# A two-block transformer kernel: the value product of the cross-attention moved behind the query product with the softmax inside it, and a one-block product that keeps its own bank parity

## What is computed

```python
def memory_cross_attention(hn, mem_n, w_q, w_kv, w_o):
    q = (hn @ w_q).reshape(B, S, CROSS_HEADS, CROSS_HEAD)
    k, v = split_cols_2(mem_n @ w_kv, (CROSS_HEADS * CROSS_HEAD, CROSS_HEADS * CROSS_HEAD))
    ...
    s = jnp.einsum('bshd,bmhd->bhsm', q, k).astype(jnp.float32) * (CROSS_HEAD ** -0.5)
    prob = jax.nn.softmax(s, axis=-1).astype(v.dtype)
    o = jnp.einsum('bhsm,bmhd->bshd', prob, v).reshape(B, S, CROSS_HEADS * CROSS_HEAD)
    return o @ w_o
```

## Time and profile before

| | |
|---|---|
| median of 3 runs | 2597.48 us (2597.47 to 2599.82) |
| the profiled execution | 2600.32 us, of which its span in the trace is 2598.5 us |
| PE busy | 2432.8 us, 94% of the span |
| DVE, ACT busy | 1391.4 us (54%), 1097.9 us (42%) |
| mean granted clock of PE | 0.964 of full speed |
| memory traffic | 492.46 MB read, 191 GB/s over the span |

### The profile page before, as it was taken

How to read it: one execution, slowest core, us unless ns; L and a number is a source line. 1 busy time by engine, 2 the same in 40 slices (tenths; PEclk the granted TensorE clock), 3 DMA queues, 4 the chain that set the end, 5 groups by cost and what they waited for, 6 DMA issues and landing times.

```text
span 2598.5 us, 29841 instructions
## 1 busy us (share of the span) xinstructions
PE 2432.8 (94%) x12196; PEld 1935.8 (74%) x12196; DVE 1391.4 (54%) x1302; ACT 1097.9 (42%) x1106; POOL 45.0 (2%) x74
## 2 busy tenths in 40 slices
PE   5799999999989899999999887999899999999996
PEld 0486778887568788877877666787788888888885
DVE  0245345456936787566456765654545545445443
ACT  1355535343334444545344623345534434434332
POOL 0000000001000000000000000000000000000000
PEclk7799999999989999999999988999999999999998
DMA  9945445557956596654555001554455555555552
GB/s 390 369 145 191 149 134 164 176 189 293 420 216 228 202 381 214 209 178 155 175 178 162 27 17 30 212 183 156 130 188 185 184 194 189 189 193 185 193 194 98
DMA packets 231536, 498.00 MB, mean 192 GB/s; under 512 B 29240, under 2 KB 31304, under 8 KB 222064
## 3 DMA queue, kind: packets, MB, share of 16 engines
q1 hardware_dynamic: 224976, 459.44, 52.0%
q0 software_dynamic: 6432, 36.72, 3.8%
HBM read 492.46 MB, written 3.67 MB: 191 GB/s over the span
## 4 chain that ended last, share of the span: by engine, by line
PE 63%; DVE 5%; ACT 2%; DMA 2%; issue 1%; DVEq 0%; POOL 0%; ACTq 0%
PE banks L2325 55%; PE banks L2395 2%; DMA raw_eight<-in_w_ada 1%; PE banks L2692 1%; ACT weights_hi L718 1%; DVE weights_lo L1378 1%; PE banks L2751 1%; PE banks L2570 1%; PE banks L2533 1%; DVE inverse_products L2109 1%; PE banks L2516 0%; DVE inverse_by_chunk L2110 0%; DVE residual L1731 0%; DVE residual L1736 0%; PE banks L2666 0%
## 5 line engine op out<-in xcount | busy, mean ns | idle before, releaser
L1378 DVE TENSOR_TENSOR weights_lo<-weights_raw,weights_hi 128x2048 fp32r<-128x2048 f32 (+1 forms) x364 | 816.5, 2244 | 899.1 <-ACT weights_hi L718 896.6
L718 ACT ACTIVATE weights_hi<-weights_raw 128x2048 fp32r<-128x2048 f32 (+1 forms) x364 | 683.3, 1878 | 1062.3 <-PE banks L2325 1045.0
L2325 PE MATMUL banks<-weights_hi,acts_hi 128*128 128x512 f32 (+1 forms) x2240 | 887.7, 396 | 31.7 <-ACT gate_rank_T L731 10.1
L2325 PE MATMUL banks<-weights_lo,acts_hi 128*128 128x512 f32 (+1 forms) x2240 | 876.0, 391 | 0.0
L2325 PE MATMUL banks<-weights_hi,acts_lo 128*128 128x512 f32 (+1 forms) x2240 | 875.7, 391 | 0.0
L2325 PEld LDWEIGHTS banks<-weights_hi,acts_hi 128*128 128x128 f32 x2240 | 424.5, 190 | 135.2 <-issue 27.7
L2325 PEld LDWEIGHTS banks<-weights_hi,acts_lo 128*128 128x128 f32 x2240 | 424.3, 189 | 88.3
L2325 PEld LDWEIGHTS banks<-weights_lo,acts_hi 128*128 128x128 f32 x2240 | 425.0, 190 | 85.7 <-issue 1.2
L2325 PE MATMUL banks<-weights_hi,hidden_hi 128*128 128x512 f32 x320 | 124.9, 390 | 0.0
L2325 PE MATMUL banks<-weights_hi,hidden_lo 128*128 128x512 f32 x320 | 124.5, 389 | 0.0
L2325 PE MATMUL banks<-weights_lo,hidden_hi 128*128 128x512 f32 x320 | 124.5, 389 | 0.0
(11 more groups left out here) (503 smaller groups left out, 1947.0 us busy)
## 6 DMA issues: line engine op xcount, KB each, us to landing
weights_raw<-in_w_in_e SPq DMA_DIRECT2D x80, 1024.0 KB, 5.3
raw_eight<-in_w_ada SPq DMA_DIRECT2D x72, 1024.0 KB, 16.0
weights_raw<-in_w_up SPq DMA_DIRECT2D x64, 1024.0 KB, 5.7
weights_raw<-in_w_down SPq DMA_DIRECT2D x64, 1024.0 KB, 5.1
weights_raw<-in_w_in SPq DMA_DIRECT2D x44, 1024.0 KB, 5.1
weights_raw<-in_w_in_o SPq DMA_DIRECT2D x32, 1024.0 KB, 5.7
weights_raw<-in_w_out_e SPq DMA_DIRECT2D x16, 1024.0 KB, 5.4
gate_chunks<-in_w_ada POOLq DMA_DIRECT2D x16, 1024.0 KB, 7.6
```

Source lines behind the costliest of these rows:

```text
L718: eng.activation(WHI[:, c % 2, :, 0:n], RAW[:, sl, :, 0:n], ACT.Copy).then_inc(hi_ready, 1)
L1378: eng.tensor_tensor(WLO[:, c % 2, :, 0:n], RAW[:, c % 4, :, 0:n], WHI[:, c % 2, :, 0:n].bitcast(F32), ALU.subtract).then_inc(lo_ready, 1)
L2325: ins = eng.matmul(BANKS[:, par * 2 + h, 0:s.n], x[:, t, h * P:(h + 1) * P], w[:, c % 2, k, 0:s.n], start=(kc == 0 and k == 0 and m == 0), ...
```

## The change

It is made of two parts.

**Block numbers.** A stage is still rounded up to an even number of blocks where its end would be odd, except `att1`, `cross_k` and `cross_q`. `lora` now is an odd block, in banks 2 and 3, and `rkv` starts with an even one. No instruction moves by this on any engine; only banks and semaphore counts differ.

**Cross-attention.** `cross_kv` is cut into `cross_k` and `cross_v`, and `cross_q` stands between them. The transposes of K stay inside `cross_q`. Those of Q, all four units of scores and the transposes of the first two units of probabilities stand on PE inside `cross_v`, the softmax on ACT and DVE there too. Behind `cross_v` remain two units of transposes, all four products with V, and their split. `cross_probs_T` has a slot for each unit, and the four small buffers stand elsewhere.

```diff
@@ stages
-        Stage("cross_kv", wv(a["w_kv_cross"][0], 0, D, 0, NB), 2, x=(XTH2, XTL2), acts="memT", scale=2, dest=lambda b, h: CKV[:, bass.ds(b, 1), h, :]),
+        Stage("cross_k", wv(a["w_kv_cross"][0], 0, D, 0, NB), 1, loop=False, x=(XTH2, XTL2), acts="memT", scale=2,
+              dest=lambda b, h: CKV[:, 0, h, :]),
         Stage("cross_q", wv(a["w_q_cross"][0], 0, D, 0, NB), 1, loop=False, acts="x3T", scale=4, ahead=2, dest=lambda b, h: CQ[:, 0, h, :]),
+        Stage("cross_v", wv(a["w_kv_cross"][0], 0, D, NB, NB), 1, loop=False, x=(XTH2, XTL2), acts="memT", scale=2, ahead=2,
+              dest=lambda b, h: CKV[:, 1, h, :]),
...
-        b += s.nblk + s.nblk % 2
+        s.pad = 0 if s.name in ("att1", "cross_k", "cross_q") else (b + s.nblk) % 2
+        b += s.nblk + s.pad
...
-                        evac(s, b, b % 2)
+                        evac(s, b, (s.b0 + b) % 2)
@@ ACT
-        stream(st["cross_q"], after={3: lambda: (rms_squares(XN, 4, Y), tiles_out("ckT", CKT))})
-        tiles_out("cqT", CQT)
+        stream(st["cross_q"], after={0: x3_hi(4, 5), 1: x3_hi(6, 7), 3: lambda: (rms_squares(XN, 4, Y), tiles_out("ckT", CKT))},
+               following=st["cross_v"])
...
+        stream(st["cross_v"], after={1: lambda: tiles_out("cqT", CQT), 2: lambda: units(cross_exp, 0, 1),
+                                     3: lambda: (units(cross_exp, 2, 3), units(cross_probs_copy, 0, 1))}, hold=True)
+        values_out = held.pop()
+        hi(st["cross_o"], st["cross_o"].g0, 0, 0)
+        values_out()
+        units(cross_probs_copy, 2, 3)
+        units(cross_hi, 0, 1, 2, 3)
+        stream(st["cross_o"])
@@ DVE
+        stream(st["cross_q"], after={0: x3_lo(4, 5), 1: x3_lo(6, 7), 3: lambda: inverse_rms(4)}, following=st["cross_v"])
+        lo(st["cross_v"], st["cross_v"].g0, 0, 1)
...
+        stream(st["cross_v"], after={2: lambda: (units(cross_max, 0, 1), units(cross_divide, 0, 1)),
+                                     3: lambda: (units(cross_max, 2, 3), units(cross_divide, 2, 3))})
+        lo(st["cross_o"], st["cross_o"].g0, 0, 0)
+        units(cross_lo, 0, 1, 2, 3)
@@ PE
-        stream(st["cross_kv"], after={1: x3_tiles(0, 1, 2, 3), 3: x3_tiles(4, 5), 4: x3_tiles(6, 7)})
+        stream(st["cross_k"], after={1: x3_tiles(0, 1, 2, 3), 2: x3_tiles(4, 5), 3: x3_tiles(6, 7)})
...
+        stream(st["cross_v"], after={0: cross_queries, 1: all_scores, 2: lambda: units(cross_probs, 0, 1)})
+        units(cross_probs, 2, 3)
+        eng.wait_ge(block_out, 4 + 2 * st["cross_o"].b0)
+        units(cross_outputs, 0, 1, 2, 3)
```

More of the change, by code:

```diff
@@ L737, in evac @@
                 eng.activation(s.dest(i, h), src, func, scale=scale)\
-                   .then_inc(block_out, 3 if h == 1 and s.nblk % 2 else 1)
+                   .then_inc(block_out, 3 if h == 1 and s.pad else 1)
         held = []
@@ L1313, in _ @@
                                  10: memory_hi(0, 1), 11: memory_hi(2, 3), 12: memory_hi(4, 5), 13: memory_hi(6, 7)})
[L1314 to L1317 removed]
+        stream(st["cross_k"], after={2: lambda: rms_squares(MEMN, 2, Y), 3: x3_hi(0, 1, 2, 3)}, following=st["cross_q"])
+        stream(st["cross_q"], after={0: x3_hi(4, 5), 1: x3_hi(6, 7), 3: lambda: (rms_squares(XN, 4, Y), tiles_out("ckT", CKT))},
+               following=st["cross_v"])
         def cross_exp(u):
@@ L1332, in cross_probs_copy @@
         def cross_probs_copy(u):
-            if u >= 2:
-                bank_full(eng, J[f"cross_o{u - 2}"])
             jj = J[f"cross_p{u}"]
             bank_full(eng, jj)
-            free(eng.activation(CPT[:, u % 2, :], bank(jj), ACT.Copy), jj)
+            free(eng.activation(CPT[:, u, :], bank(jj), ACT.Copy), jj)
         def cross_tiles(t, u):
@@ L1347, in cross_hi, with units @@
             ch.done("cross_hi")
-        def cross_attention():
-            for step, u in ((cross_exp, 0), (cross_exp, 1), (cross_exp, 2), (cross_probs_copy, 0), (cross_exp, 3),
-                            (cross_probs_copy, 1), (cross_probs_copy, 2), (cross_hi, 0), (cross_probs_copy, 3),
-                            (cross_hi, 1), (cross_hi, 2), (cross_hi, 3)):
-                step(u)
-        stream(st["cross_o"], after={0: cross_attention})
+        def units(step, *us):
+            return [step(u) for u in us]
+        stream(st["cross_v"], after={1: lambda: tiles_out("cqT", CQT), 2: lambda: units(cross_exp, 0, 1),
[6 more added lines that the diff above has]
+        stream(st["cross_o"])
         first_up = st["up0"]
@@ L2241, in _ @@
                       10: memory_lo(0, 1), 11: memory_lo(2, 3), 12: memory_lo(4, 5), 13: memory_lo(6, 7)}, hold=True)
-        second = st["cross_q"]
-        stream(st["cross_kv"], after={2: lambda: inverse_rms(2), 3: x3_lo(0, 1, 2, 3), 5: x3_lo(4, 5), 6: x3_lo(6, 7)},
-               following=second)
-        lo(second, second.g0, 0, 1)
-        stream(st["cross_q"], after={3: lambda: inverse_rms(4)})
+        stream(st["cross_k"], after={2: lambda: inverse_rms(2), 3: x3_lo(0, 1, 2, 3)}, following=st["cross_q"])
+        lo(st["cross_q"], st["cross_q"].g0, 0, 1)
+        stream(st["cross_q"], after={0: x3_lo(4, 5), 1: x3_lo(6, 7), 3: lambda: inverse_rms(4)}, following=st["cross_v"])
+        lo(st["cross_v"], st["cross_v"].g0, 0, 1)
         def cross_max(u):
@@ L2358, in stream @@
                 acts_ready(s, kt)
-                chunk(s, None, b % 2, kc, g, g, kt, s.kc)
+                chunk(s, None, (s.b0 + b) % 2, kc, g, g, kt, s.kc)
                 if c in after:
@@ L3005, in _, with cross_queries @@
         stream(st["cross_q"], after={1: cross_keys})
-        eng.wait_ge(block_out, 4 + 2 * st["cross_o"].b0)
-        transposes("cqT", natural(CQ))
-        jobs_out(eng, "cqT")
+        def cross_queries():
+            eng.wait_ge(block_out, 4 + 2 * st["cross_v"].b0)
+            transposes("cqT", natural(CQ))
         def cross_scores(u):
@@ L3036, in cross_outputs, with units, all_scores @@
                     ins = eng.matmul(bank(jj)[:, e * P:(e + 1) * P], CKV[:, 1, sh, g * P:(g + 1) * P],
-                                     CPT[:, u % 2, (2 * e + sh) * P:(2 * e + sh + 1) * P], start=(sh == 0),
+                                     CPT[:, u, (2 * e + sh) * P:(2 * e + sh + 1) * P], start=(sh == 0),
                                      stop=(sh == 1))
             full(ins, jj)
-        for u in range(4):
-            cross_scores(u)
-        for step, u in ((cross_probs, 0), (cross_probs, 1), (cross_probs, 2), (cross_outputs, 0), (cross_probs, 3),
-                        (cross_outputs, 1), (cross_outputs, 2), (cross_outputs, 3)):
-            step(u)
+        def units(step, *us):
+            return [step(u) for u in us]
+        def all_scores():
+            jobs_out(eng, "cqT")
+            units(cross_scores, 0, 1, 2, 3)
+        stream(st["cross_v"], after={0: cross_queries, 1: all_scores, 2: lambda: units(cross_probs, 0, 1)})
+        units(cross_probs, 2, 3)
+        eng.wait_ge(block_out, 4 + 2 * st["cross_o"].b0)
+        units(cross_outputs, 0, 1, 2, 3)
         stream(st["cross_o"], after={2: x4_tiles(0, 1), 3: x4_tiles(2, 3)})
```

26 lines of the change are left out of this document (10 added, 16 removed).

## The result

The changed kernel takes **2583.79 us** (median of four runs, 2582.68 to 2586.69) against 2597.83 us for the kernel before on the same chip (2597.47 to 2599.82): ratio 0.9946, 95% interval 0.9929 to 0.9963. The gain is 14.0 us where 18.2 were forecast; the range of 2577 to 2585 holds the time. The profiled execution took 2586.69 us with a span of 2584.9 us, against 2598.5 before: 13.6 us.

What follows compares the result with a forecast made beforehand. PE, busy for 94% of the span, was taken as the bound, so only its idle or slow time counts. Gains of 8.45 and 9.7 us sum to 18.2, from 2597.5 to 2579.3 us; range 2577 to 2585.

Steps and rivals of the forecast that it cites:

- The two stops: PE's waits from `att1` to `lora` and `lora` to `rkv`: removing them and the slow matmuls behind gains 8.45 us.
- the sign: Between `lora` and `rkv`: `rkv`'s first matmul starts within 0.8 us of `lora`'s last, at full speed.
- The replaced 22.2 us: PE's stretch from `cross_q` to `cross_o`: 22.2 us give way to 12.5 us, a gain of 9.7 us.
- The wait ahead of `cross_v`: Ahead of `cross_v`'s first chunk PE waits 0.6 us for K's copies and the split.
- Q's transposes: Eight transposes of Q between the chunks of `cross_v` cost PE 0.9 us.
- scores: The 16 records of scores on PE inside `cross_v` cost 3.7 us, as they stand.
- probabilities: Transposes of two units of probabilities on PE cost 0.9 us.
- the end: Behind `cross_v`: V's copy with eight transposes, 32 records of products with V and the last split cost 6.4 us.
- The softmax not hidden: Exponentials hold up a split in `cross_v` and PE waits: 2582.5 to 2584.5 us, both failures 2586; chance 0.07.
- one part brings nothing: Either part fails: 2587.8 us without the first, 2589.0 without the second; chance 0.05.
- The clock falling inside `cross_v`: Short transposes and scores between `cross_v`'s chunks let the clock fall: 28 us more, 2607 us; chance 0.04.
- the gain is given back: At a later wait that doesn't move with PE, the gain is lost: 2597.5 us; chance 0.03.

Runs made afterwards that it cites:

- the block numbers' kernel: Kernel before with the change's block numbers alone, cross-attention as before: 2592.75 us, ratio 0.9979; run once more, 2592.83 us, ratio 0.9967.
- the single filler: Changed kernel plus one fp32 128x512 matmul on constants behind the second half of the corner products, ahead of the solve: 2578.5 us, ratio 0.9913.
- the changed kernel's second run: The changed kernel once more, nothing altered, in a later group: 2585.34 us, ratio 0.9936 to the kernel before.
- 5.4 with three: Changed kernel plus three fp32 128x512 matmuls on constants, one and two behind the halves of the corner products: 2580.51 us, ratio 0.9927.
- 9.1 with three in the kernel before: Kernel before plus three filler matmuls, one behind the first and two behind the second half of the corner products: 2597.51 us, ratio 0.9988.

## Why the prediction was right, and where it was off

**The two stops: right.** Forecast 8.45 us, measured 8.41 less the 0.29 that lay ahead, 8.1. The first stop went whole (0.23 us from start to start), at the second 0.49 us of idle time stayed for `weights_lo` where 0.56 was forecast, and that split was indeed what is late next. `rkv` starts 0.81 us behind `lora`'s last matmul, at the edge of the 0.8 that the sign allowed.

**The replaced 22.2 us: right, and by its terms.** The wait ahead of `cross_v` 0.6 (1786.36 less 1785.54 and 0.23; forecast 0.6), Q's transposes 0.87 (0.9), scores 3.45 (3.7), probabilities 0.87 (0.9), the end 6.54 (6.4: V's copy 1.52, products 3.84, last split 1.18). Sum 12.3 where 12.5 stood; the lead grew by 10.1 us where 9.7 stood. The softmax hid with 1.3 us of room at V's fourth chunk where 1.6 was forecast.

**The rivals.** The softmax not hidden did not come; the experiment with the softmax behind V shows what the cover is worth, 6.6 us. That one part brings nothing is excluded by the two kernels with one part each (6.4 and 11.2 us). The clock falling inside `cross_v` did not come: 1.00 from 1786 to 1820 us. For that rival the Trainium skill ("TensorE: Matmul & The Clock Gate", "A second HAM failure mode: psum-queue depth-cycling") was weighed; by that rule the stretch would have run partly low. It didn't; but the rows above show no idle moment between its groups, so the rule's condition was not met, and this run says nothing against it.

**What was off: the sum.** It added the two local gains and took all that lies behind as unchanged: "the gain is given back" had a chance of 0.03, because I looked for "no long stop of PE behind either place". The loss is no stop. It is a stretch of PE work that runs at the lower clock level for longer, 4.8 us from R0 to the first `a_rb_T` product (leads 8.26 and 3.47), some 300 us behind the first place. The other terms, 8.1 and 10.1 us, give with the 0.3 us that lay ahead of the change 18.5; less 4.8 this is 13.7, and 13.6 were measured in the spans. The forecast's time was therefore 4.5 us low, and its bounds of 2577.8 to 2583.4, made of the bounds of the local terms alone, missed the 2583.79; the range held it by luck, because it reached out for another rival.

Could it have been seen in the trace of before? The prediction says of the clock: "I see it fall only behind stops near 3 us". That reading was wrong. The windows behind the first place are:

```profile
1440.00:1500.00 60.00, 50.30 (x233) 35.44 (x231) 45.88 (x84) 35.39 (x68) 1.07 (x2) 0.88 0.04 12
1500.00:1560.00 60.00, 52.56 (x376) 40.39 (x376) 35.71 (x65) 19.62 (x43) 5.25 (x2) 0.84 0.08 18
1560.00:1620.00 60.00, 46.65 (x700) 38.00 (x701) 35.42 (x74) 23.98 (x63) 1.89 (x2) 0.89 0.14 33
```

Ahead of the solve it fell at 1604.5 us, in an idle time of 1.52 us, with none above 0.70 us in the 20 us before; from 1659 to 1663 us it is at 0.57 with PE recorded busy for all 4.00 us. The rows also have the place: the clock at 0.56 and 0.58 from 1604 to 1612 us, and then the 96 records of small matmuls of the solve. They don't say that the low stretch would last 20 us if it began 10 us earlier. But a cost for "the low stretch there gets longer" could have been bounded: with every small matmul at half the clock, by this estimate at most their 5.9 us once more. That bound was missing.

**What stays open.** Why the low stretch lasts some 20 us where R0 starts 4.88 to 5.16 us behind the fall, and 7 or 10 us where it starts earlier or later, the runs do not tell; only that PE was recorded busy for all of 1604 to 1612 us in both executions of the block numbers' kernel. The Trainium skill ("TensorE: Matmul & The Clock Gate", "What's actually happening") says that the monitor behind the clock runs free and doesn't start anew with a kernel, so that the place of a change of level differs between executions. The two executions of one program agree with that: R0 starts 5.38 us behind the fall in one and 4.88 in the other. Nor is it settled how much of the 6.8 us in the medians is the single filler's. Its trace, set against that of the changed kernel's second run, gains 5.6 us up to the first `a_rb_T` product, loses 1.5 again ahead of the memory's transposes, and gains 1.6 between 1870 and 1901 us. The last is the clock again, far from the filler; these are the windows of the changed kernel's second run and of the one with a filler:

```profile
1870.00:1874.00 4.00, 4.00 (x13) 3.12 (x12) 0.74 (x1) 0.00 (x0) 0.00 (x0) 0.60 0.97 334
1870.00:1874.00 4.00, 4.00 (x19) 3.34 (x18) 2.05 (x1) 1.92 (x1) 0.00 (x0) 1.00 0.38 146
```

Both traces of the block numbers' kernel are without that loss too, and no run tells whether the filler had a part in it.

## What to carry to other kernels

Sum the local gains of a change, and then look at each later stretch in which PE runs small matmuls around a fall of the granted clock: where such a stretch lies against the clock's steps can cost or return several microseconds, here 3.3 between two executions of one program and 4.8 of some 18 that the edit brought. If a program's times fall into two groups, compare a trace of each before explaining the median. A full-width matmul on constants put into an existing wait of PE (here 1.69 us, ahead of the solve) cost 0.2 us of lead, took the stretch from R0 to the state product from 13.27 to 8.48 us, and came with a median 6.8 us lower, half of what the whole change brought. It is worth a try beside such a stretch. That it makes times steadier is not shown: they spread over 2.4 us with one filler, 5.4 with three, and 9.1 with three in the kernel before.
